# A five-stage transformer front end in split float32: where the rotary angles, pool groups, low parts, dilated scores and last heads are placed

## The reference, cut to what matters

```
for layer in (0, 1):
    h += 0.5 * rms_norm(swiglu(rms_norm(h)))        # ffn(layer, 0)
    h += rms_norm(mixer(rms_norm(h)))               # layer 0: pool, layer 1: dilated
    h += 0.5 * rms_norm(swiglu(rms_norm(h)))        # ffn(layer, 1)
    after layer 0: k, v = shared_kv(h)              # rope(norm(h) @ w_k), norm(h) @ w_v
pool(x):    u = x @ w_in; per group of 256 channels, window w = 2, 4, 8, 16:
            p = mean of the last w tokens of u - u
            y = (p @ w_group per group) * scale @ w_out
dilated(x): q = rope(x @ w_q); 3 head groups (dilation 1, 4, 16), 8 heads each,
            banded softmax, the groups joined by their log-sum, @ w_o
rope:       angle = position * inv_freq; cos and sin of it
```

## Time and profile before

| what | value |
|---|---|
| time, median of 3 runs | 3629.45 us (3626.37 to 3630.61) |
| the profiled execution's own time | 3632.27 us |
| its span, first to last instruction | 3630.3 us |
| PE, DVE, ACT, POOL busy | 89%, 48%, 32%, 34% |
| mean granted TensorE clock | 0.943 of full speed |
| first five stages and ffn(1,1) | to about 2165 us of the span |

### The profile page before, as it was taken

How to read it: one execution, slowest core, us unless ns; L and a number is a source line. 1 busy time by engine, 2 the same in 40 slices (tenths; PEclk the granted TensorE clock), 3 DMA queues, 4 the chain that set the end, 5 groups by cost and what they waited for, 6 DMA issues and landing times.

```text
span 3630.3 us, 53848 instructions
## 1 busy us (share of the span) xinstructions
PE 3244.4 (89%) x20644; PEld 2434.3 (67%) x20644; DVE 1747.4 (48%) x3135; ACT 1146.8 (32%) x1963; POOL 1216.3 (34%) x998
## 2 busy tenths in 40 slices
PE   7999889999899998998899988788979878688787
PEld 5888668777678776776678766555756655455454
DVE  4343765334634364444524366553653266554534
ACT  3222333212422132112312233443434234444343
POOL 3444444444344432222344444311331233213211
PEclk9999999999999999999999989988989988898889
DMA  3222222433233321111233321000101111001011
GB/s 134 93 98 97 77 82 82 139 122 110 100 126 107 133 81 64 53 59 47 81 133 110 122 105 36 25 19 24 36 14 64 47 53 36 30 25 36 24 53 41
DMA packets 74356, 264.66 MB, mean 73 GB/s; under 512 B 7856, under 2 KB 9136, under 8 KB 73904
## 3 DMA queue, kind: packets, MB, share of 16 engines
q1 hardware_dynamic: 67104, 242.25, 19.4%
q10 hardware_dynamic: 7056, 19.69, 1.5%
HBM read 252.47 MB, written 7.34 MB: 72 GB/s over the span
## 4 chain that ended last, share of the span: by engine, by line
PE 71%; DVE 15%; issue 7%; ACT 4%; POOL 2%; DMA 0%; ACTq 0%; DVEq 0%; POOLq 0%
PE ps L1320 53%; PE ps L1815 2%; PE ps L1836 2%; PE ps L1788 2%; POOL wl L855 1%; PE ps L1398 1%; DVE work L2071 1%; DVE tb L2473 1%; PE ps L1681 1%; DVE tb L2118 1%; PE ps L1623 1%; PE ps L1379 1%; PE ps L1641 1%; DVE hc L1984 1%; PE ps L1701 1%
## 5 line engine op out<-in xcount | busy, mean ns | idle before, releaser
L855 POOL TENSOR_TENSOR wl<-raw,wh 128x1024 fp32r<-128x1024 f32 x320 | 791.8, 2474 | 1220.6 <-ACT wh L966 705.4
L1320 PE MATMUL ps<-xh,wh 128*128 128x512 f32 x2400 | 916.2, 406 | 97.5 <-POOL wl L843 30.9
L1320 PE MATMUL ps<-xl,wh 128*128 128x512 f32 x2400 | 864.5, 385 | 0.0
L1320 PE MATMUL ps<-xh,wl 128*128 128x512 f32 x2400 | 862.8, 384 | 0.0
L1320 PEld LDWEIGHTS ps<-xh,wh 128*128 128x128 f32 x2400 | 442.8, 196 | 277.9 <-issue 155.5
L966 ACT ACTIVATE wh<-raw 128x1024 fp32r<-128x1024 f32 x224 | 237.6, 1061 | 982.4 <-PE ps L1320 934.0
L843 POOL TENSOR_TENSOR wl<-raw,wh 128x1024 fp32r<-128x1024 f32 x90 | 220.3, 2448 | 918.0 <-ACT wh L944 918.0
L1320 PEld LDWEIGHTS ps<-xl,wh 128*128 128x128 f32 x2400 | 443.1, 196 | 93.3 <-issue 13.1
L1320 PEld LDWEIGHTS ps<-xh,wl 128*128 128x128 f32 x2400 | 441.2, 195 | 87.6
L1320 PE MATMUL ps<-ah,wh 128*128 128x512 f32 x1104 | 437.5, 403 | 25.4 <-issue 14.2
L1320 PE MATMUL ps<-al,wh 128*128 128x512 f32 x1104 | 420.5, 388 | 0.0
(11 more groups left out here) (348 smaller groups left out, 3625.3 us busy)
## 6 DMA issues: line engine op xcount, KB each, us to landing
raw<-wts_dram SPq DMA_DIRECT2D x458, 512.0 KB, 3.4
spilled_dram<-hc ACTq DMA_DIRECT2D x1, 3072.0 KB, 8.7
hc<-spilled_dram ACTq DMA_DIRECT2D x1, 3072.0 KB, 12.8
tb<-tab_dram ACTq DMA_DIRECT2D x5, 512.0 KB, 3.7
hc<-x_dram ACTq DMA_DIRECT2D x8, 256.0 KB, 9.2
spilled_dram<-hc ACTq DMA_DIRECT2D x1, 2048.0 KB, 7.2
hc<-spilled_dram ACTq DMA_DIRECT2D x1, 2048.0 KB, 9.3
out_dram<-hc SPq DMA_DIRECT2D x8, 256.0 KB, 2.1
```

The costliest lines, as they stand in the source:

```text
L855: pool.tensor_tensor(wl[:, n % SPLIT, :], raw[:, LOADED[n] % RAW, :], wh[:, n % SPLIT, :].bitcast(F32), ALU.subtract).then_inc(lo_done, 1)
L1320: ins = pe.matmul(out_, w[:, s, k * P:(k + 1) * P], x_(k, at), start=first, stop=last)
```

## The change

- **Rotary angles one stage up.** `rope_tables()` runs at the start of ffn(0,1) instead of ffn(1,0), in `tb` instead of `fo`; the positions' DMA is issued at the end of `pool` and the `keep` stage is gone. ACT's Sin stay where they were.
- **Pool.** The group products come after all input tiles; the first uses banks 4 to 7, the second banks 0 to 3, the output tiles begin at bank 4 and no longer wait for `taken`. POOL makes the low part of an input tile after the next tile's remainder.
- **add_f.** `x_low(k-1)` stands ahead of the add of slice k.
- **kv_low** is spread: parts 0 to 2 after tile 1 is taken, 3 and 4 after its `finish`, 5 to 7 after tile 2 is taken.
- **Dilated events.** For a v tile the first event follows quarter 2 instead of quarter 1.
- **Last heads last.** The output projection starts when three of four head pairs are in; its first tile goes by k (head pair) outermost and waits for the last pair before k = 3. Each tile signals its first half (`half_full`), and DVE copies, ACT squares and DVE adds half by half.

```diff
-POOL_TILES = [..., ("in", 2), ("in", 3), ("group", 2), ("in", 0), ("in", 1), ("group", 0)]
+POOL_TILES = [..., ("in", 2), ("in", 3), ("in", 0), ("in", 1), ("group", 2), ("group", 0)]
@@ dilated_steps
-        if part % 2:
+        if part == 3 or part == 1 and what != "v" or part == 2 and what == "v":
             event()
@@ POOL (gpsimd), pool
+                    late = []
                     for what, m in POOL_TILES:
                         remainder(c.at("tile"))
                         c.take("tile")
-                        if what == "in":
+                        for k in late:
                             pool.wait_ge(part_hi, c.take("part") + 1)
-                            pool.tensor_tensor(alk(m), tt[:, m % 2, :], ahk(m).bitcast(F32), ALU.subtract).then_inc(a_ready, 1)
-                        else:
-                            c.take("part", 4)
+                            pool.tensor_tensor(alk(k), tt[:, k % 2, :], ahk(k).bitcast(F32), ALU.subtract).then_inc(a_ready, 1)
+                        late = [m] if what == "in" else []
+                    c.take("part", 8)
@@ ACT, pool (was keep) and dilated
                 f_rstd()
-
-            def keep():
                 act.dma_start(t1[:, 1, :].bitcast(I32), pos).then_inc(cond_in, 16)
...
                 for m in range(0, KC, 2):
+                    act.wait_ge(half_taken, m // 2 + 1)
+                    f_square(m)
                     n = tile()
                     act.wait_ge(taken, n + 5)
-                    f_square(m), f_square(m + 1)
+                    f_square(m + 1)
@@ PE, pool
-                    if g0 == 0:
-                        pe.wait_ge(x_ready, x0 + 4)
+                    pe.wait_ge(taken, n + (3 if g0 == 0 else 1))
...
-                    pe.wait_ge(taken, n + 1)
...
-                        ins = mm3([ps[:, n % 4, :]], ...)
+                        ins = mm3([ps[:, pool_bank(m), :]], ...)
@@ PE, dilated
-                wait_a(A_HEADS // 2)
+                wait_a(A_HEADS // 2 - 1)
                 settle()
+                c.take("a")
                 for m in range(0, KC, 2):
                     n, bb = pair()
-                    for b in range(2):
-                        for k in range(4):
-                            ...
-                    ins.then_inc(tile_done, 1)
+                    for b, k in [(b, k) for k in range(4) for b in range(2)] if m == 0 else [(b, k) for b in range(2) for k in range(4)]:
+                        if (m, b, k) == (0, 0, 3):
+                            pe.wait_ge(a_ready, c.at("a"))
+                        ...
+                        if k == 3:
+                            ins.then_inc(tile_done if b else half_full, 1)
@@ DVE, add_f
                     own(dve.scalar_tensor_tensor(t, fo[:, k, :], gain(k), r, ALU.mult, ALU.mult))
+                    if k and name != "ada":
+                        x_low(k - 1, gain_of(name, *at))
                     give(dve.tensor_tensor(hc[:, k, 0:SEQ], hc[:, k, 0:SEQ], t, ALU.add), h_ready, "h")
                     if name == "ada":
                         modulated(at[0], k)
-                    elif k:
-                        x_low(k - 1, gain_of(name, *at))
@@ DVE, ffn_phase
-                if (layer, i) == (1, 0):
+                if (layer, i) == (0, 1):
                     rope_tables()
@@ DVE, dilated
                         if at[0] == DILATED_TILES[1]:
-                            kv_low()
+                            kv_low(0, 1, 2)
+                        if at[0] == DILATED_TILES[2]:
+                            kv_low(5, 6, 7)
                     elif step == "finish":
                         finish(*at)
+                        if at[0] == DILATED_TILES[1]:
+                            kv_low(3, 4)
...
-                        add_square(m - 2), add_square(m - 1)
+                        add_square(m - 1)
+                    b = 2 * (c.at("tile") % 2)
+                    dve.wait_ge(half_full, m // 2 + 1)
+                    dve.tensor_copy(fo[:, m, :], ps[:, b, :]).then_inc(half_taken, 1)
+                    dve.wait_ge(half_taken, m // 2 + 1)
+                    add_square(m)
                     n = tile()
-                    b = 2 * (n % 2)
-                    took(dve.tensor_copy(fo[:, m:m + 2, :], ps[:, b:b + 2, :]), n)
-                add_square(KC - 2), add_square(KC - 1)
+                    took(dve.tensor_copy(fo[:, m + 1, :], ps[:, b + 1, :]), n)
+                add_square(KC - 1)
```

More of the change, by code:

```diff
@@ L47 @@
 POOL_READY = {2: 4, 3: 2, 1: 6, 0: 8}
-POOL_TILES = [("in", 6), ("in", 7), ("in", 4), ("in", 5), ("in", 2), ("in", 3), ("group", 2), ("in", 0), ("in", 1), ("group", 0)]
+POOL_TILES = [("in", 6), ("in", 7), ("in", 4), ("in", 5), ("in", 2), ("in", 3), ("in", 0), ("in", 1), ("group", 2), ("group", 0)]
 LEVELS = 7
@@ L640, in tokens @@
             return SEQ if layer == DEPTH - 1 and what in "qgm" else TOK
-        PHASES = [("ffn", 0, 0), ("pool",), ("ffn", 0, 1), ("keep",), ("ffn", 1, 0), ("dilated",), ("ffn", 1, 1)]
+        PHASES = [("ffn", 0, 0), ("pool",), ("ffn", 0, 1), ("ffn", 1, 0), ("dilated",), ("ffn", 1, 1)]
         for layer in range(DEPTH):
@@ L1026, in ffn @@
                         get(d2a, "d2a")
-                        act.activation(cs1[:, s, :], fo[:, 4 + s, :], ACT.Sin).then_inc(tables_ready, 1)
+                        act.activation(cs1[:, s, :], cs1[:, s, :], ACT.Sin).then_inc(tables_ready, 1)
                 for number, part in enumerate(FF_PARTS):
@@ L1060, in pool @@
                         for b in group_blocks(m):
-                            act.activation(ahk(2 * m + b), ps[:, 4 + b, :], ACT.Copy, scale=col("pscale", 2 * m + b)).then_inc(part_hi, 1)
+                            act.activation(ahk(2 * m + b), ps[:, group_bank(m, b), :], ACT.Copy, scale=col("pscale", 2 * m + b)).then_inc(part_hi, 1)
                 for m in range(KC):
@@ L1298, in _ @@
             hi(0), hi(1)
-            run = dict(ffn=ffn, pool=pool, keep=keep, dilated=dilated, ada=ada_phase, mixers=mixers, mix=mix)
+            run = dict(ffn=ffn, pool=pool, dilated=dilated, ada=ada_phase, mixers=mixers, mix=mix)
             for name, *rest in PHASES:
@@ L1494, in pool @@
                             for w, x_, first, last in ((wh, a_hi, k == 0, False), (wh, a_lo, False, False), (wl, a_hi, False, k == 1)):
-                                ins = pe.matmul(ps[:, 4 + b, :], w[:, n % SPLIT, blk * P:(blk + 1) * P], x_(2 * g + k, 0), start=first, stop=last)
+                                ins = pe.matmul(ps[:, group_bank(g0, b), :], w[:, n % SPLIT, blk * P:(blk + 1) * P], x_(2 * g + k, 0), start=first, stop=last)
                     ins.then_inc(tile_done, 1)
@@ L1895, in _ @@
             get(a2p, "a2p")
-            run = dict(ffn=ffn, pool=pool, keep=lambda: None, dilated=dilated, ada=lambda layer: None, mixers=mixers, mix=mix)
+            run = dict(ffn=ffn, pool=pool, dilated=dilated, ada=lambda layer: None, mixers=mixers, mix=mix)
             for name, *rest in PHASES:
@@ L2144, in rope_tables @@
                 dve.wait_ge(cond_in, 32)
-                ang, u, v = (fo[:, k, :] for k in range(3))
-                own(dve.tensor_copy(fo[:, 3, :], t1[:, 1, :].bitcast(I32)))
-                own(dve.tensor_scalar(ang, fo[:, 3, :], const("invf"), None, ALU.mult))
+                u, ang = t1[:, 0, :], t1[:, 1, :]
+                own(dve.tensor_copy(u, t1[:, 1, :].bitcast(I32)))
+                own(dve.tensor_scalar(ang, u, const("invf"), None, ALU.mult))
                 for s in range(2):
+                    v = cs1[:, s, :]
                     own(dve.tensor_scalar(u, ang, 1.0 / (2 * math.pi), 0.25 if s == 0 else 0.0, ALU.mult, ALU.add))
@@ L2155, in rope_tables @@
                         own(dve.tensor_scalar(v, v, math.pi / 2, None, ALU.add))
-                    give(dve.tensor_scalar(fo[:, 4 + s, :], v, PI_IN, -PI_IN, ALU.min, ALU.max), d2a, "d2a")
+                    give(dve.tensor_scalar(v, v, PI_IN, -PI_IN, ALU.min, ALU.max), d2a, "d2a")
             def dilated():
@@ L2218, in end, with kv_low @@
                     split(t1[:, 1, :], ahk(KC + hp), alk(KC + hp), a_ready, "a")
-                def kv_low():
-                    for k in range(KC):
+                def kv_low(*some):
+                    for k in some:
                         dve.wait_ge(part_hi, c.take("part hi") + 1)
                         dve.scalar_tensor_tensor(alk(k), h0(k), col("kv", k), ahk(k).bitcast(F32), ALU.mult, ALU.subtract).then_inc(a_ready, 1)
-                    c.take("a", KC)
+                    c.take("a", len(some))
                 wait_rs()
@@ L2583, in _ @@
             c.take("h", KC)
-            run = dict(ffn=ffn_phase, pool=pool, keep=lambda: None, dilated=dilated, ada=lambda layer: None, mixers=mixers, mix=mix)
+            run = dict(ffn=ffn_phase, pool=pool, dilated=dilated, ada=lambda layer: None, mixers=mixers, mix=mix)
             for name, *rest in PHASES:
```

19 lines of the change are left out of this document (12 added, 7 removed).

## The result

The changed kernel took 3601.82 us (median of 6 runs, 3598.36 to 3610.55) where before took 3627.91 (6 runs, 3623.22 to 3637.29): a ratio of 0.9929, 95% interval 0.9912 to 0.9946. The gain of 26.1 us stands beside the forecast one of 26.8. The profiled execution took 3601.33 us with a span of 3599.3. Two executions further down, one of e5 (13773.51 us) and one of before beside e10 (8727.42), took over twice as long as the others and are left out of the ratios and of the time given for e5.

The account below looks back on a forecast made before the run. PE, busy 89% of the span, was taken as the bound, with gains only in its waits and low clock. Terms summed to 26.8 us: 3632.27 became 3605.5 profiled, 3602.7 on the median; range 3592 to 3615.

Parts of the forecast that it names:

- the next add 4.2 after the last matmul: Sign of being right: behind the output projection, the next add starts 4.2 us after PE's last matmul.
- The low clock where no wait is over 2 us: Sign of being wrong: PE's clock drops to the 1.2 GHz level where no wait exceeds 2 us.
- Angles into ffn(0,1), -7.5: Rotary angles at ffn(0,1)'s start delay its fourth tile, tile 3, and bring low clock: 7.5 us lost, bounds 3.4 to 8.6.
- Angles out of ffn(1,0), +6.7: Without the angles at ffn(1,0)'s start, its tiles 2 and 3 start sooner: 6.7 us gained, 5.5 to 8.7.
- the rival built on it: ACT stands still behind its table loads in ffn(1,0), the skill page's rule: 4.1 us less gain, 3606.8, chance 0.02.
- add_f, 0.7 at each of three joints: Low part ahead of the add starts pool, dilated and ffn(1,1) 0.7 us sooner each: 2.1 us gained.
- Pool, +0.7: In pool, group products last let PE go on at 480.1 to 481.5: 0.7 us gained, between -0.7 and +1.6.
- kv_low, +3.8: In dilated, spreading the low parts removes PE's 4.18 us wait before the third tile's half-turn: 3.8 us gained, 3.0 to 6.0.
- Scores, 7.5 and 2.3 for the clock: In dilated, scores a quarter later shorten nine PE waits: 7.5 us (5 to 10), plus 2.3 (0 to 3.1) from clock.
- the rival of a low clock through all of dilated: More but shorter PE waits keep the low clock through the three head-pair rounds: slower, up to 3678 us, chance 0.03.
- Last heads last, +7.0: Output projection's first tile no longer waits 4.04 us and keeps full clock: 7.0 us gained, 3.6 if low clock comes.
- half by half, +4.2: Projection halves leave only the last slice to copy, square and sum at the end: 4.2 us gained, 2.5 to 5.0.

Follow-up runs that it names:

- e5: Changed kernel with the projection's first output tile back behind all four head pairs in its old order, halves kept: 3611.54 us, ratio to before 0.9946.
- e10: Changed kernel with the edits of e3 and e8 together: 3596.26 us, ratio to before 0.9899.
- e0: The changed kernel itself run again, as the base for stage lengths: 3610.32 us, ratio to before 0.9935.
- e1: Changed kernel with only the rotary angles back at the head of ffn(1,0): 3612.47 us, ratio to before 0.9940.
- e7: Changed kernel with the old order in add_f, a slice's add ahead of the previous slice's low part: 3611.23 us, ratio to before 0.9940.
- e8: Changed kernel with pool's low part of an input tile right behind that tile's own remainder again: 3607.44 us, ratio to before 0.9922.
- e6: Changed kernel with all eight kv_low parts in one place again, ahead of tile 1's last rope piece: 3608.58 us, ratio to before 0.9943.
- e4: Changed kernel with the scores event one quarter earlier again, after parts 1 and 3: 3619.86 us, ratio to before 0.9964.
- e3: The kernel of e2 with each projection slice's square added on DVE one copy later: 3601.37 us, ratio to before 0.9914.
- e9: Changed kernel with both halves of a projection tile copied and squared at once again, heads still last: 3612.28 us, ratio to before 0.9932.
- e2: Changed kernel with the angles in ffn(0,1) moved behind its first part's gate and up tiles: 3601.42 us, ratio to before 0.9907.

## Why the prediction was right

It held as a whole (26.1 measured, 26.8 forecast) and stage by stage within 0.9 us in the profiled pair. The closeness is luck in part: against e0, the same kernel, the two ffn stages are 2.3 and 1.8 off, and in dilated misses cancel (the halves 2.0 and `kv_low` 0.8 too large, the scores 1.3 and `add_f` 1.7 too small). What holds beyond that are the chains. Of the signs that were set, PE's wait of 5 to 6, tile 2 near 21, no idle time before L1649 (L1641 before), and 14.3 down to 3.1 with new waits of 0.3 and 0.45 came; the next add 4.2 after the last matmul did not (6.10). The low clock where no wait is over 2 us, a sign of being wrong, is there behind the 1.83 late in ffn(0,1), but before has it at the same place. The terms fared unevenly.

- **Angles into ffn(0,1), -7.5:** the stage gave -7.7. The chain is the one described; the wait was 5.79, forecast some 6. e1 puts the angles' own price at 10.4, some 1.5 of it chance: before and after have half the clock behind the 1.83 wait late in the stage (0.57 over 4 us), and e1 has the full one. That chance is also why -7.7 and 10.4 can both stand; the rest of the distance, 1.2, fits `add_f`'s own gain, which -7.7 has in it. The angles start 1.0 late behind the reordered `add_f`, where 0.7 was counted.
- **Angles out of ffn(1,0), +6.7:** 6.5. Tile 2 starts 21.1 us behind the stage's first matmul, forecast 21. The next operation behind a table load started within 0.02 us of its end once more, with three loads in 6 us:
```profile
959.98 1.28 ACT L989 ACT_TABLE_LOAD   x1
961.28 0.66 ACT L989 ACTIVATE ps<-ps,sm 128x512 f32<-128x512 f32 x1
961.96 1.28 ACT L990 ACT_TABLE_LOAD   x1
963.25 0.60 ACT L990 ACTIVATE work<-ps 128x512 f32<-128x512 f32 x1
```
The drain of 1.38 us that the Trainium skill (ScalarE: Activation LUTs, What ACT_TABLE_LOAD costs) puts there does not show here either, and the rival built on it is out. (Its sum, 26.8 less 4.1, is 22.7 and not the 22.6 of the prediction.)
- **add_f, 0.7 at each of three joints:** the mechanism holds, but the terms were sized as if the order did nothing else. By e7 it gives 0.5 into pool, 2.4 into dilated (with the clock), and costs where DVE has a list of its own behind the last low part. Over the four stages e7 takes 1312.4, between the 1309.0 and 1312.8 of the changed kernel's two profiles: in the sum nothing is left that the profiles can tell from zero. As e7 alone of the three has the full clock behind the late 1.83 in ffn(0,1), the gain can as well be some 1 to 5 us. The share of ffn(1,1) was not separated from the variation of the rest.
- **Pool, +0.7:** 0.7 (1.2 in the profiled pair) with `add_f`'s 0.5 taken off, and PE goes on at 480.79, forecast 480.1 to 481.5. The size was right, and its parts were not looked at: the low part behind a remainder of 2.4 stands in the prediction's chain, but not as a cost of its own. By e8 this one move costs 4.2 (some 3.9 against the first profile), so that the group order and its banks are worth some 4.6 (133.56 less 128.43 less 0.5). The prediction's list of idle stretches leaves out six waits of PE in pool for POOL's remainders, 0.34 to 2.90 us and 7.5 in all; they became 7.1, so nothing of the sum hung on them.
- **kv_low, +3.8:** 3.0 by e6. The wait did not vanish, as I had said; 1.83 of it stayed.
- **Scores, 7.5 and 2.3 for the clock:** 11.1 by e4, at the upper part of the bounds. Of the nine waits, the five of 1.9 became 0.54 to 0.56, the one of 1.58 some 0.2 and the three of 1.05 nothing, with new waits of 0.3 before the rows where I had allowed 0.3 to 0.8 for the maximum. Half the clock is gone from 1380 to 1680, and with it the rival of a low clock through all of dilated.
- **Last heads last, +7.0, and half by half, +4.2:** the two together gave 9.2 of 11.2 (from the end of the last values to the next multiply: 37.3 before, 28.1 after). The first tile lost its wait and its low clock, 6.9 us by the last matmul. The step that failed is that of the halves: I took the 4.2 of pool's end over, where DVE is idle between tiles. Here it runs copy, wait for ACT, add, for each half, with one add in two held beside POOL, and is behind PE by the time of the last; the distance was 6.10. e3 shows that the order of copies and adds held it, and gets the 4.2. That the two terms are not independent is what e5 (1.25 lost again) and e9 (3.2) show.

What the forecast missed is small in its sum, but two improvements lay there, 4.2 us in pool and 1.9 at the end of the projection, and a third, some 9, in the place of the angles. e8, e3 and e2 took them.

## What to carry to other kernels

Price a move of a block of work by what stands behind it on its engine: the same 17 operations cost some 8 to 12 us ahead of a take that PE waits for (7.7 from before to after, 8.8 to 12.5 by e1 and e2 against the two profiles of the changed kernel, of which some 1.5 is the clock), and nothing where PE had free banks to fill while they ran. When a shared engine has two pieces to do, the one whose reader asks first goes first, whatever order the loop suggests (4.2 us in pool). When two edits feed the same tail, price the tail once with both in, and check that its engine is idle before the last piece, or else the time saved ahead of it is only lent.

## What the runs showed that I had not expected

- **The same wait does not always bring the low clock.** Behind the 1.83 us wait late in ffn(0,1) the clock was half in eight of the thirteen profiles (before, after, e0, e4, e5, e6, e9, e10) and full in five (e1, e2, e3, e7, e8), with PE's work and waits around it alike. The same wait in ffn(1,0) was followed by the full clock in six (before, after, e0, e5, e6, e7) and by half in seven. What decides it no run here shows. One such spell costs some 1.5 us, and the spells at the joints vary too: in the two profiles of the changed kernel the clock turned full 7.5 and 9.4 us behind the multiply ahead of ffn(1,0). That makes stages of one kernel differ by 2 to 3 us, and is the reason why single terms were read from waits and distances and not from totals.
- **A very short operation can be held for as long as a long one.** Timeline of DVE and POOL in the changed kernel's pool stage:
```profile
466.21 2.24 DVE L2136 TENSOR_TENSOR work<-tb,cn 128x16 f32<-128x16 f32 x1
```
```profile
465.63 2.78 POOL L850 TENSOR_TENSOR wl<-raw,wh 128x1024 fp32r<-128x1024 f32 x1 [1.93 <-ACT wh L952]
```
This operation on 16 elements of each partition took 2.24 us and ended 0.04 after POOL's remainder; in e8, where the remainder fell elsewhere, the same operation took 0.17. By the Trainium skill (SBUF — State Buffer, Who interferes with whom) an operation of VectorE that needs the port pair it shares with GpSimd is blocked outright until the other's instruction ends, so that its own size doesn't matter; the trace agrees.
